# Two PSUM banks for the products of values, and two in place of three for the ring of scores, turned queries and index products

## The reference

```python
logits = jnp.einsum('bqhd,bsd->bqhs', qib, k_idx) * IDX_SCALE
score = jnp.einsum('bqh,bqhs->bqs', wb, jax.nn.relu(logits))
score = jnp.where(causal[None], score, -jnp.inf)
_, sel = lax.top_k(score, n_keep)
...
s = jnp.einsum('bqgrd,bqkgd->bqgrk', qg, kg) * ATTN_SCALE
s = jnp.where(valid[:, :, None, None, :], s, -jnp.inf)
pr = jax.nn.softmax(s, axis=-1)
o = jnp.einsum('bqgrk,bqkgd->bqgrd', pr, vg)
```

## Time and profile before

| | us |
|---|---|
| median of 3 runs | 3249.56 |
| lowest, highest | 3245.02, 3249.63 |
| the profiled execution | 3245.62 |
| its span, first to last instruction | 3243.8 |
| TensorE busy | 2958.4 (91%) |
| VectorE busy | 1719.7 (53%) |
| ScalarE busy | 1384.8 (43%) |
| GpSimd busy | 390.2 (12%) |

### The profile page before, as it was taken

The page is one execution under the profiler, slowest core; times in us unless marked ns, Lnnn a source line. Parts: engine busy times, 40 slices in busy tenths (PEclk is TensorE's granted clock), DMA queues, the critical chain, the costliest instruction groups (busy, mean ns, idle before and its releaser), DMA issues.

```text
span 3243.8 us, 37680 instructions
## 1 busy us (share of the span) xinstructions
PE 2958.4 (91%) x14264; PEld 2407.2 (74%) x14264; DVE 1719.7 (53%) x3405; ACT 1384.8 (43%) x2202; POOL 390.2 (12%) x447
## 2 busy tenths in 40 slices
PE   5999977788788898899699999999999999999987
PEld 4887755566666676787588888888888888888875
DVE  3376778686777776832333344533445334453344
ACT  3252546575747547655322243322433224332232
POOL 1233331213040040000000001000010000100001
PEclk9999988889897887899899999999999999999998
DMA  3111142111110110111424233333323333233321
GB/s 122 61 49 54 38 126 69 36 59 44 40 50 28 41 41 11 45 33 43 149 91 134 94 117 104 117 126 102 117 97 124 124 104 117 92 130 123 103 92 39
DMA packets 224627, 266.50 MB, mean 82 GB/s; under 512 B 58176, under 2 KB 160320, under 8 KB 224448
## 3 DMA queue, kind: packets, MB, share of 16 engines
q1 hardware_dynamic: 222144, 255.72, 25.0%
q10 hardware_dynamic: 2304, 8.39, 0.6%
HBM read 224.07 MB, written 40.01 MB: 81 GB/s over the span
## 4 chain that ended last, share of the span: by engine, by line
PE 79%; DVE 7%; issue 7%; ACT 4%; POOL 2%; DMA 1%; SPq 0%; DVEq 0%; ACTq 0%; POOLq 0%
PE bank L1732 58%; PE bank L1874 6%; PE bank L1854 6%; PE bank L1754 3%; PE bank L1840 2%; PE bank L1755 2%; ACT kept L968 2%; DVE kept L1346 1%; PE bank L1703 1%; DVE probs L1484 1%; ACT probsT L1071 1%; POOL score L868 1%; DVE too_few L1354 1%; DMA w_in_raw<-in_w_in 1%; ACT score_tail L968 0%
## 5 line engine op out<-in xcount | busy, mean ns | idle before, releaser
L1554 DVE TENSOR_TENSOR w_lo<-w_raw,w_hi 128x1024 fp32r<-128x1024 f32 x296 | 361.5, 1222 | 582.2 <-ACT w_hi L1114 582.1
L1114 ACT CAST w_hi<-w_raw 128x1024 fp32r<-128x1024 f32 x296 | 308.5, 1043 | 661.4 <-PE bank L1732 641.5
L1854 PE MATMUL bank<-values,probsT 128*128 128x64 f32 x2176 | 335.3, 301 | 150.9 <-ACT probsT L1071 124.2
L1854 PEld LDWEIGHTS bank<-values,probsT 128*128 128x128 f32 x2176 | 314.6, 220 | 177.3 <-ACT probsT L1071 163.6
L1732 PE MATMUL bank<-hn_hi,w_hi 128*128 128x512 f32 x1024 | 400.2, 391 | 20.8 <-DVE hn_lo L1574 20.8
L1732 PE MATMUL bank<-hn_hi,w_lo 128*128 128x512 f32 x1024 | 398.9, 390 | 0.0
L1732 PE MATMUL bank<-hn_lo,w_hi 128*128 128x512 f32 x1024 | 398.9, 390 | 0.0
L1732 PE MATMUL bank<-w_hi,hid_hi 128*128 128x512 f32 x1024 | 398.7, 389 | 0.0
L1732 PE MATMUL bank<-w_hi,hid_lo 128*128 128x512 f32 x1024 | 398.4, 389 | 0.0
L1732 PE MATMUL bank<-w_lo,hid_hi 128*128 128x512 f32 x1024 | 398.4, 389 | 0.0
L1484 DVE CUSTOM_DVE_ANT_0 probs<-bank,mask 128x384 f32<-128x384 f32 (+3 forms) x320 | 193.7, 607 | 234.3 <-PE bank L1755 232.5
(11 more groups left out here) (200 smaller groups left out, 4983.1 us busy)
## 6 DMA issues: line engine op xcount, KB each, us to landing
w_raw<-in_w_up SPq DMA_DIRECT2D x64, 1024.0 KB, 5.7
w_raw<-in_w_down SPq DMA_DIRECT2D x64, 1024.0 KB, 5.0
w_raw<-in_w_ple_gate SPq DMA_DIRECT2D x16, 1024.0 KB, 5.1
x_in<-in_x SPq DMA_DIRECT2D x16, 512.0 KB, 3.6
q_t<-q_scratch SPq DMA_DIRECT2D x32, 256.0 KB, 3.7
x_t<-in_x SPq DMA_DIRECT2D x16, 512.0 KB, 4.3
h_scratch<-h_t SPq DMA_DIRECT2D x16, 512.0 KB, 2.9
hnT_scratch<-hn2T_t SPq DMA_DIRECT2D x16, 512.0 KB, 3.8
```

What stands on the lines that cost most here:

```text
L1114: nc.scalar.copy(piece_parts(p, w_hi[:, p % 4, :]), raw_piece(p)).then_inc(w_hi_rdy, 1)
L1554: nc.vector.tensor_tensor(piece_parts(p, w_lo[:, p % 4, :]), raw_piece(p), piece_parts(p, w_hi[:, p % 4, :]).bitcast(F32), ALU.subtract).t ...
L1854: last = nc.tensor.matmul(bank[:, 4, h * HEAD:(h + 1) * HEAD], probsT[:, m % 3, a * P:(a + 1) * P], values[:, kt, HEAD * kv:HEAD * (kv + 1 ...
```

## The change

Three things, all in the attention stage. The ring deals out banks 6 and 7 alone. Bank 5, so freed, takes the products of values of odd tiles, and bank 4 those of even tiles, in `weigh` and in the division in `outputs`. And the first product of values of tile i waits, from tile 2 on, for the division of tile i - 2, the last that read the same bank, in place of tile i - 1. The order of instructions is the same on every engine.

```diff
         for item in [("q", 0, 0), ("q", 0, 1)] + [("s", *x) for x in steps[:head_first[2]]]:
-            place(item, (6, 7, 5), n)
+            place(item, (6, 7), n)
             n += 1
         for m in range(len(steps)):
             for item in ([("s", *x) for x in score_at[m]] + [("q", *x) for x in q_turn_at.get(m, ())]
                          + [("qi", *x) for x in at["turn"].get(EARLY_SPOTS + m, ())]
                          + [("x", *x) for x in at["index"].get(EARLY_SPOTS + m, ())]):
-                place(item, (6, 7, 5), n)
+                place(item, (6, 7), n)
                 n += 1
...
+        def value_bank(i):
+            return 4 + i % 2
...
-                nc.vector.tensor_tensor(o_sb[:], bank[:, 4, :].rearrange("p (h d) -> p h d", d=HEAD),
+                nc.vector.tensor_tensor(o_sb[:], bank[:, value_bank(i), :].rearrange("p (h d) -> p h d", d=HEAD),
                                         over(inv_denom[:], HEAD), ALU.mult).then_inc(o_rdy, 1)
...
                 pe.wait_ge(pT_ev, m + 1)
-                if b == 0 and h == 0 and i >= 1:
-                    pe.wait_ge(o_rdy, i)
+                if b == 0 and h == 0 and i >= 2:
+                    pe.wait_ge(o_rdy, i - 1)
                 for a in range(w // P):
                     kt = o // P + a
-                    last = nc.tensor.matmul(bank[:, 4, h * HEAD:(h + 1) * HEAD], probsT[:, m % 3, a * P:(a + 1) * P],
+                    last = nc.tensor.matmul(bank[:, value_bank(i), h * HEAD:(h + 1) * HEAD], probsT[:, m % 3, a * P:(a + 1) * P],
                                             values[:, kt, HEAD * kv:HEAD * (kv + 1)], start=(kt == 0), stop=(kt == i))
```

## The result

| | before | changed | changed, second series |
|---|---|---|---|
| median, us | 3249.56 (3 runs) | 3281.38 (3 runs) | 3284.59 (4 runs; before beside it 3248.39) |
| ratio to before, 95% interval | | 1.0100 [1.0081, 1.0120] | 1.0114 [1.0096, 1.0132] |
| profiled execution, its span | 3245.62, 3243.8 | 3281.76, 3280.0 | 3281.41, 3279.6 |

The changed kernel is slower, by 31.8 us in the first series and 36.2 in the second. The forecast was 3272.5 us, +22.9, with 3252 to 3292 as its range.

A forecast was written before the change was run, and what follows sets the result against it. TensorE was taken to bound the index stretches, VectorE the picking stretches, and both to be full from 1340 to 1380. 18.7 + 2.0 + 3.2 + 2.5 - 3.5 = +22.9 us, giving 3272.5 us, range 3252 to 3292.

The forecast's parts named there:

- The index steps: Steps with index products, TensorE the bound: two ring banks delay 35 steps, 21.2 us less 2.5, taken as +18.7 us.
- Rival 2: Index steps bound by VectorE or GpSimd absorb the delay: +9 us in total, 3258; chance 0.10 above 3256.
- the 2.5 absorbed: At 938.71 TensorE's wait of 2.46 us for a copy behind GpSimd's late root shrinks: 2.5 us off the index loss.
- It does not come back: Index steps: TensorE's 0.66 us lost in a step stays lost, and the next step loses its 0.6 afresh.
- Rival 3: Index stretches: short waits bring the clock down, up to +43 us beside the 23, 3316; chance 0.12.
- The picking steps: Steps with VectorE the bound: raw delays up to 3.4 us counted as nothing, except at two places where TensorE is full afterwards.
- +2.5 for the clock: Clock fall after the new wait at 1365: half of 5 us at the lower clock counted as lost, +2.5 us.
- At 1365: Picking, at 1365.59: a score block waits for a bank whose reading stands behind VectorE's scan, +3.2 us.
- At 728.89: Picking: a score block waits for a bank that VectorE frees at 730.9, after a split of index queries, +2.0 us.
- TensorE later waits less: Picking steps: ground for counting raw delays up to 3.4 us as nothing while VectorE is the bound.
- The waits for o_sb: Products of values at changes of tile: of 26.1 us waited, -3.5 taken; three long waits, 13.1, count 0; far end -18.1.
- Rival 1: Waits for o_sb worth the 18.1 us shown, ring costs no more than 10: -8 us, 3241; chance 0.06.

The follow-up runs named there:

- the run with three items: Kernel before, with three of 482 ring items taking the bank of the item two back, all others keeping three banks: 3258.84 us, ratio 1.0031.

## Why the prediction was right, and where it was off

**The index steps** (18.7 taken). Measured by the run with two banks there alone: +18 to +20 us. The mechanism is shown: the delay of a step is mostly 0.65 to 0.7 us (VectorE's readings in the earlier trace rows follow each other at 0.66 us, not at the 0.69 that the prediction names), and it comes afresh in each step of a stretch. Rival 2, by which GpSimd or VectorE would absorb it, is out as a whole: that would have been +7. But the close agreement is in part luck. The prediction had 2.4, 2.2, 3.8, 4.1 (6.6 less the 2.5 absorbed) and 6.2 us for the five stretches. In the profile of that run four of them lose 2.7, 3.3, 5.0 and 7.5, 18.5 us where 14.6 were taken, and the one that is left, steps 117 to 128, loses 3.5 that are gone again by step 166. In the changed kernel the same happens to 4.6 us. "It does not come back" is right inside a stretch and failed for this one. What gave the time back stays open: in steps 128 to 166 the clock was at 1.2 GHz for 55 to 61 us in the kernels whose ring was changed, and for 65 us in both profiles of the kernel before, so it can be the clock as well as slack.

**The clock in the index steps.** It stayed at 1.00, 1.00, 0.96 and 1.00 although TensorE now pauses about twice a step. Rival 3 is out (its sum also took +43 us, the 180 us less the 136.6 of work, where the stretches themselves would grow from 143 to 180, by 37): pauses of 0.5 to 0.6 us in a step of 3.4 to 4.2 us did not lower the clock. What the section of the Trainium skill quoted with it (page "TensorE: Matmul & The Clock Gate") tells of another kernel did not happen in this one.

**The picking steps** (+2.0, +3.2 and +2.5 for the clock; 7.7 together). This is the step that failed by size: the rest of the ring measures +14 to +16 us. At 1365 the wait for the scan came (2.4 us in the changed kernel, 3.0 in the run with three items), and the low clock behind it. The stretch loses 5.9 us for 5.7 taken, but the terms differ: the wait makes 2.6 to 3.3 us (3.2 taken), the step behind it, with the projection at the low clock, 1.1 to 1.7 (2.5 taken), and the steps with three short waits for the ring between 1375 and 1387, which were counted at nothing, 1.6. That the total fits is luck. At 728.89, +2.0 was taken, and the ring alone shows 1.7. What was missed stands at two places. In steps 107 to 117 turned index queries wait 2.8 us behind VectorE: +2.2 us with the ring of two alone, +0.9 in the changed kernel. And at 554 to 560 it is 5.3 us, 3.9 after what comes back by step 32. The prediction had the raw delay of 3.4 us in its list and counted nothing, because VectorE was the bound there and "TensorE later waits less". The step that failed is that inference: beside VectorE's scan TensorE was doing work that VectorE needed afterwards, the output projection of 3.60 us ahead of the next score block. A delay of TensorE is free while VectorE is the bound only as long as what TensorE puts off is still done before VectorE runs out of work. The timeline of the changed kernel shows it (PE is TensorE, DVE VectorE):

```profile
553.83 0.97 PE L1821 MATMUL bank<-ident,q_t 128*128 128x128 f32 x4 [2.37 <-DVE block_max L1487]
...
559.92 1.09 PE L1769 MATMUL bank<-ident,qi_t 128*128 128x128 f32 x4 [2.53 <-DVE block_max L1487]
...
560.79 5.30 PE L1877 MATMUL bank<-wo_sb,mixT_t 128*128 128x512 f32 x8
...
566.71 0.69 DVE L1487 CUSTOM_DVE_ANT_0 probs<-bank,mask 128x512 f32<-128x512 f32 x1 [3.10 <-PE bank L1758]
```

**The waits for o_sb** (-3.5 taken, -18.1 at the far end). The reasoning for the three long ones holds: their 13.1 us did not come back. At 547, 715 and 1113 (in the time of the kernel before) TensorE reached the step 3.6, 6.8 and 3.5 us earlier than the step before would have let it, and within five steps had lost it all again, to the ring and to ScalarE (at 1113 but for 0.9 us, by which the ring of two alone was ahead there as well). For 715:

```profile
719.50 0.50 PE L1757 MATMUL bank<-k_parts,q_hi 128*128 128x512 f32 x1 [2.44 <-DVE block_max L1487]
...
722.29 0.69 DVE L1500 TENSOR_TENSOR o_sb<-bank,inv_denom 128x512 f32<-128x512 f32 x1
...
723.51 0.69 PE L1757 MATMUL bank<-k_parts,q_hi 128*128 128x384 f32 x1 [1.84 <-DVE block_max L1487]
...
731.64 1.97 PE L1857 MATMUL bank<-values,probsT 128*128 128x64 f32 x8 [2.72 <-ACT probsT L1074]
```

But the short ones brought no gain in total either. Of the three comparisons two go the wrong way by a few us, the change against the ring of two alone (31.8 and 36.2 against 30.8 us) and the second value bank against its control, both with two banks for turned probabilities (+5.4); the third, the kernel whose values and ring share four banks against the kernel before, gives -0.2, where -3.5 is not excluded. Rival 1 is out. The term of -3.5 is not supported by any pair. In that third kernel the wait for ScalarE's copy grew by nearly what the wait for o_sb had been, so in those steps ScalarE's own queue was the next thing late.

The profiles show where the gain went. Against the ring of two alone the changed kernel is 1.1 us shorter in steps 27 to 32 and 1.3 in steps 107 to 117, but 2.2 and 3.0 us longer in steps 62 to 69, around the longest wait. Steps 62 to 69 are longer in the other two pairs as well, by 1.1 and 2.4 us. There the prediction had 0, on the ground that VectorE is full. It is not full any more: TensorE and ScalarE, rearranged, come late for it. VectorE's idle time in these steps grows from 0.4 us with the ring of two alone to 2.4 and 2.7 in the changed kernel, from 0.8 before to 1.9 in the third kernel, and from 0.2 to 2.6 in the last pair, nearly as much as the steps grow.

**The sum.** The terms as measured are 18 to 20 and 14 to 16, with 0 for the second value bank: +32 to +36. The forecast's +22.9 lacks the 3.9 us of one place, the 1 to 2 us of steps 107 to 117, and 3.5 us of gain that was not there; with these it would be +31 to +33.

What stays open is why VectorE waits longer in steps 62 to 69 with a second bank for values. TensorE comes out of the place of the old wait up to 6.8 us ahead and is then held by the ring and by ScalarE, three shorter waits in place of one long one. The clock stood at 1.2 GHz there for 17 to 19 us in all executions with a second value bank, and for 7 to 14 us in those without, but for one: the kernel with a ring of four, with 17 us, one value bank, two waits of VectorE in the same places (1.25 and 1.11 us) and 2.3 us more than its control. That speaks for the clock as what makes TensorE late; no run separates it from the order of the waits.

## What to carry to other kernels

A wait's length in a profile is what the waiting engine loses there, not what the kernel loses. Before freeing it, look at who is late: if that engine is full for the next steps, the wait moves to the next thing that it has to deliver, and the rearranged engines can come late for the full one in turn. Before taking a buffer out of a ring, compare for each item the end of the reading one place nearer with the item's start: where the producer is the bound, as TensorE in the index steps here, the largest positive difference of a step is paid in each step of the stretch, since the consumer's own waiting sets it up afresh. Whether it is still missing at the end of the stretch behind has to be looked up: here it was in four of five. And a delay beside a full engine is only free if the delayed engine's queue holds nothing that the full one needs next.

## What the runs showed of the hardware

TensorE paused 0.48 and 0.58 us in index steps of 3.4 to 4.2 us and kept the granted clock of 1.00 for stretches of 33 and 52 us. Waits of 2.4 to 3.4 us were followed by stretches of 3 to 10 us at 1.2 GHz (granted clock 0.50), and the same eight products of the projection, which lay partly or wholly in them, took 4.42 to 5.48 us in place of 3.60 and 3.65. One execution of the kernel before repeated the first within 0.7 us in every stretch of the attention stage, although its times over 17 executions lie between 3243.74 and 3254.35 us. Two executions of the changed kernel differed by 7 us in one search stretch and by 5 in another, so a difference of that size in one stretch of one profile is not yet a finding.
